# Forgetting attention scores: the product with the keys' rests over 128 partitions in place of 64

## The chip, the cores and the metric
The kernel runs on one core of one Trainium2 chip. The metric is the device time of one execution in microseconds (us), from runs of the whole program; a profile of one further execution shows where the time goes.

## What is computed
The program is a whole small model: a block of forgetting attention ("Fox") with a convolutional feed-forward part, a block of HGRN2 with another, and a second model of retention, stick-breaking attention and a gated feed-forward part. All arithmetic is asked in float32. The change concerns the Fox scores alone:

```python
q = rms_norm(q, q_gain) * hd ** -0.5        # 16 heads of 64, 528 tokens
k = rms_norm(k, k_gain)
s = jnp.einsum('bqhd,bkhd->bhqk', q_blk, k)
s = s + c_blk[..., None] - c[:, :, None, :]
s = jnp.where(q_pos[:, None] >= key_pos[None, :], s, -jnp.inf)
p = jax.nn.softmax(s, axis=-1)
o = jnp.einsum('bhqk,bkhd->bqhd', p, v)
```

## The kernel before
**Splitting.** TensorE takes its operands in a rounded float32 form (fp32r), so a float32 number is kept as a rounded part and a rest, and a dense product is the sum of three: rounded with rounded, rounded with rest, rest with rounded. For the dense layers ScalarE rounds each weight tile (`act_hi`, L404) and VectorE subtracts (`dve_lo`, L408); `pe_group` then issues 48 matmuls for each group of 8 tiles (L445, 128 rows by 128 columns stationary, 264 columns moving; L441 in later stages with 512 columns moving).

**A pair of heads.** The Fox stage runs over 8 pairs of heads. Queries and keys of a pair stand as 128 partitions: head 0 in the lower 64, head 1 in the upper 64. `q_p[:, b, :]` holds for head b its rounded queries on the head's own 64 partitions and their rests on the other 64 (`query_parts`, L1814 to L1821, VectorE). `k_p[:, b, :]` holds the rounded keys of head b on both halves (`key_parts`, L1240, four copies on ScalarE recorded at L1146). So one product over 128 partitions gives (rounded query + query rest) times rounded key. `k_l` holds the rests of the keys (`key_rest`, L1823 to L1827, VectorE), each head's on its own half.

**The scores of a head.** `scores(i, b)` (L753) makes 17 matmuls: for five blocks of query rows (four of 128, one of 16) the product with `k_p` at L766 over 128 partitions, the product with `k_l` at L768 over the 64 partitions of the head, and one at L770 that adds the mask on the diagonal. The last block's keys are split in two runs. The lengths of the moving operand are 128, 256, 384 and 512 for the full blocks, and 128 and 400 for the last. TensorE issues a weight load with every matmul, whether or not the stationary operand is the same as before.

**Order.** TensorE runs a pair as: transposes of the values (L696), dense group 0 of the next pair, `scores(i, 0)`, group 1, `scores(i, 1)`, group 2, `turned(0)` (transposes at L780), group 3, `fox_out(0)` (L684, L688), `turned(1)`, sums for the norms (`fox_sums`, L749), `fox_out(1)`. The last pair has one dense group in all, after both heads' scores. VectorE reads the scores from PSUM, adds the decay and finds each row's minimum (`least`, L1860), ScalarE takes the exponential (L1274), and VectorE normalises (L1872) and empties PSUM (L1877). At a pair's end VectorE scales the next queries and keys (`qk_scaled`, L1811), makes `q_p`, gates the output (`o_t`, L1914 and L1915), then makes `k_s` and `k_l`, and at last the output's rest (`yl`, L1921). ScalarE makes `k_p`, then the rounded output (`yh`), then the transposed values (`v_t`, L1146), then rounds the next weights. `scores(i, 0)` waits for `k_p`, `k_l`, `v_t` and the output of the pair before (semaphores `qk_hi`, `qk_lo`, `vt_ready`, `o_done`). Each engine takes its instructions in the order written.

Of the kernel before, what the change touches and what calls it, by code (L numbers as in the profile page):

```python
# [15 lines left out]
F32 = mybir.dt.float32  # L16
F32R = mybir.dt.float32r
BF16 = mybir.dt.bfloat16
U8 = mybir.dt.uint8
ALU = mybir.AluOpType  # L20
# [3 lines left out]
P = 128  # L24
# [3 lines left out]
L = SEQ + META  # L28
# [8 lines left out]
FOX_H, FOX_D = 16, 64  # L37
# [128 lines left out]
def program(nc, ctx, dram, out):  # L166
# [53 lines left out]
    a = Area(arena, end)  # L220
# [5 lines left out]
    a = Area(arena, end)  # L226
# [12 lines left out]
    a = Area(arena, end)  # L239
# [6 lines left out]
    k_s = a.take("k_s", [P, L])  # L246
# [5 lines left out]

    a = Area(rest, end)
    q_p, k_p = (a.take(n, [P, 2, L], F32R) for n in ("q_p", "k_p"))
    k_l = a.take("k_l", [P, L], F32R)
    ident_f, future_f = (a.take(n, [P, P], F32R) for n in ("ident_f", "future_f"))

    a = Area(rest, end)
# [22 lines left out]
    a = Area(arena, end)  # L281
# [13 lines left out]
    a = Area(after_yr, end)  # L295
    b = Area(norms_at, arena)
# [18 lines left out]
    flat = ps[:, :, :].rearrange("p b n -> p (b n)")  # L315
# [4 lines left out]
    def s(name):  # L320

        if name not in sems:
            sems[name] = ctx.enter_context(nc.semaphore(name))
        return sems[name]
# [376 lines left out]
    def _(pe):  # L701
        pe.wait_ge(s("square_loaded"), 16)
        pe.wait_ge(s("m_loaded"), 32)
        for n in range(2):
            for m in range(KT):
                last = nc.tensor.transpose(ps[:, 3, P * n + META * m:P * n + META * (m + 1)],
                                           m_tok[:, n, P * m:P * (m + 1)], ident[0:META, 0:META])
        last.then_inc(s("x_t"), 1)
        for c in range(NFULL):
            pe.wait_ge(s(f"x_loaded{c}"), 16)  # L710
            for g in range(2):
                b = 2 * c + g
                if b >= 4:
                    pe.wait_ge(s("h_init"), b - 2)
                for m in range(4):
                    last = nc.tensor.transpose(ps[:, 4 + b % 4, P * m:P * (m + 1)],
                                               x_tok[:, c, P * (4 * g + m):P * (4 * g + m + 1)], ident)
# [3 lines left out]
        for l in range(2):  # L721
            last = nc.tensor.transpose(ps[:, 1 + l, 0:4 * FT], crows[0:4 * FT, l, :], ident[0:4 * FT, 0:4 * FT])
# [29 lines left out]

        def scores(i, b):  # L753

            lo, hi = FOX_D * b, FOX_D * (b + 1)
            before = 0
            for turn in TURNS:
                before += len(turn)
                if b:
                    pe.wait_ge(s("t_min"), 10 * i + before)  # L760
                for n in turn:
                    w = TOK[n]
                    at = 1024 + SCORES0[n]
                    runs = ((0, P * n + w),) if n < NFULL else ((0, P), (P, L))
                    for k0, k1 in runs:
                        nc.tensor.matmul(flat[0:w, at + k0:at + k1], q_p[:, b, P * n:P * n + w],  # L766
                                         k_p[:, b, k0:k1], start=True, stop=False)
                        nc.tensor.matmul(flat[0:w, at + k0:at + k1], q_p[lo:hi, b, P * n:P * n + w],  # L768
                                         k_l[lo:hi, k0:k1], start=False, stop=(k1 <= P * n))
                    last = nc.tensor.matmul(flat[0:w, at + P * n:at + P * n + w], ident_f[:, 0:w],  # L770
                                            future_f[:, 0:w], start=False, stop=True)
                last.then_inc(s("s_done"), 1)
# [357 lines left out]
        for m in range(4, KT):  # L1130
            pe.wait_ge(s("ff_ready"), m + 1)
            for c in range(NFULL):
                last = nc.tensor.transpose(ps[:, 4 + c, P * (m - 4):P * (m - 3)], ff[:, m, P * c:P * (c + 1)], ident)
# [557 lines left out]
    def _(dve):  # L1691
        V = nc.vector
# [116 lines left out]
        def qk_scaled(n, j):  # L1809
            dve.wait_ge(s("qn_r"), 2 * n + j + 1)  # L1810
            V.scalar_tensor_tensor((q_s, k_s)[j][:, :], qk_raw[:, j, :], gains[:, ROW_QGAIN + j:ROW_QGAIN + j + 1],  # L1811
                                   post_t[:, j, :], ALU.mult, ALU.mult).then_inc(s("qn_done"), 1)

        def query_parts(n):  # L1814

            dve.wait_ge(s("qn_done"), 2 * n + 3)
            V.tensor_copy(q_p[lo, 0, :], q_s[lo, :])
            V.tensor_copy(q_p[hi, 1, :], q_s[hi, :]).then_inc(s("qk_lo"), 1)
            dve.wait_ge(s("qk_lo"), 2 * n + 1)
            V.tensor_tensor(q_p[hi, 0, :], q_s[lo, :], q_p[lo, 0, :].bitcast(F32), ALU.subtract)  # L1820
            V.tensor_tensor(q_p[lo, 1, :], q_s[hi, :], q_p[hi, 1, :].bitcast(F32), ALU.subtract)  # L1821

        def key_rest(n):  # L1823

            dve.wait_ge(s("qk_hi"), 2 * n + 1)
            V.tensor_tensor(k_l[lo, :], k_s[lo, :], k_p[lo, 0, :].bitcast(F32), ALU.subtract)
            V.tensor_tensor(k_l[hi, :], k_s[hi, :], k_p[hi, 1, :].bitcast(F32), ALU.subtract).then_inc(s("qk_lo"), 1)  # L1827

        V.tensor_copy(ident_f[:, :], ident)
        V.tensor_copy(future_f[:, :], future)  # L1830
# [20 lines left out]
        def pair_(i, ahead_):  # L1851
            def least(b):
                dve.wait_ge(s(f"crep_loaded{b}"), 16 * i + 16)
                for turn in range(3):
                    dve.wait_ge(s("s_done"), 6 * i + 3 * b + turn + 1)
                    carry(dve, "dve_carry")
                    for n in TURNS[turn]:
                        w, k = TOK[n], P * n + TOK[n]
                        at = 1024 + SCORES0[n]
                        V.tensor_tensor_reduce(out=t_rows[0:w, b, ROWS0[n]:ROWS0[n] + k],  # L1860
                                               in0=flat[0:w, at:at + k], in1=crep[0:w, b, 0:k],
                                               scale=1.0, scalar=3e38, op0=ALU.add, op1=ALU.min,
                                               accum_out=rowmin[0:w, 5 * b + n:5 * b + n + 1]).then_inc(s("t_min"), 1)

            def normalise(b):
                dve.wait_ge(s("p_exp"), 10 * i + 5 * b + 5)
                V.reciprocal(rowinv[:, 5 * b:5 * b + 5], rowsum[:, 5 * b:5 * b + 5]).then_inc(s("fox_step"), 1)
                dve.wait_ge(s("fox_step"), 3 * i + b + 1)
                for n in range(NTT):
                    w, k = TOK[n], P * n + TOK[n]  # L1870
                    tr = t_rows[0:w, b, ROWS0[n]:ROWS0[n] + k]
                    last = V.tensor_scalar(tr, tr, rowinv[0:w, 5 * b + n:5 * b + n + 1], None, ALU.mult)  # L1872
                last.then_inc(s("p_norm"), 1)

            def evacuate(b):
                dve.wait_ge(s("pt_mm"), 2 * i + b + 1)
                V.tensor_copy(p_t[:, 512:1024], ps[:, 3, :]).then_inc(s("pt_b"), 1)  # L1877

            def gate():
                dve.wait_ge(s("gate_exp"), i + 1)  # L1880
                V.tensor_scalar(g_s[:, :], g_s[:, :], 1.0, None, ALU.add).then_inc(s("fox_step"), 1)
                dve.wait_ge(s("fox_step"), 3 * i + 3)
                V.reciprocal(g_s[:, :], g_s[:, :]).then_inc(s("gate_ready"), 1)
            if ahead_:
                split_ahead(dve, dve_lo, PH_FOX, i, 0)
                dve.wait_ge(s("qn_done"), 2 * i + 4)
                scaled_out(PH_FOX, i, 0, qk_raw[:, 0, :])
            least(0)
            if ahead_:
                split_ahead(dve, dve_lo, PH_FOX, i, 1)  # L1890
                normalise(0)
                scaled_out(PH_FOX, i, 1, qk_raw[:, 1, :])
                least(1)
                split_ahead(dve, dve_lo, PH_FOX, i, 2)
                normalise(1)
                scaled_out(PH_FOX, i, 2, v_s[:, :])
                evacuate(0)
                split_ahead(dve, dve_lo, PH_FOX, i, 3)
                scaled_out(PH_FOX, i, 3, g_s[:, :])
            else:  # L1900
                least(1)
                split_ahead(dve, dve_lo, PH_FOXG, 0, 0)
                normalise(0)
                scaled_out(PH_FOXG, 0, 0, g_s[:, :])
                normalise(1)
                evacuate(0)
            gate()
            evacuate(1)
            if ahead_:
                qk_scaled(i + 1, 0)  # L1910
                query_parts(i + 1)
            dve.wait_ge(s("o_mm"), 2 * i + 2)
            dve.wait_ge(s("gate_ready"), i + 1)
            V.tensor_tensor(o_t[:, 0:SEQ], ps[:, 5, :], g_s[:, 0:SEQ], ALU.mult)  # L1914
            V.tensor_tensor(o_t[:, SEQ:L], ps[:, 4, 496:512], g_s[:, SEQ:L], ALU.mult).then_inc(s("o_done"), 1)  # L1915
            if ahead_:
                qk_scaled(i + 1, 1)
                key_rest(i + 1)
            dve.wait_ge(s("o_done"), i + 2)
            dve.wait_ge(s("yh_ready"), i + 1)  # L1920
            V.tensor_tensor(row(yl, i), o_t[:, :], row(yh, i).bitcast(F32), ALU.subtract).then_inc(s("y_ready"), 1)  # L1921
# [425 lines left out]
```

## Time and profile before

| | us |
|---|---|
| median of 3 runs | 2983.41 |
| lowest and highest | 2978.47, 2984.93 |
| the profiled execution | 2975.36 |
| its span, first to last instruction | 2973.7 |
| TensorE matmul, busy | 2879.0 |
| TensorE weight load, busy | 2512.3 |
| VectorE, busy | 1493.8 |
| ScalarE, busy | 1122.1 |

The mean granted TensorE clock was 0.982 of full speed. Busy time of TensorE counts modelled ends of overlapping matmuls, so the distance from one matmul's start to the next one's start says more than a duration. PE is TensorE's matmul side, PEld its weight loads, DVE VectorE, ACT ScalarE. "128*128 128x264" is a stationary operand of 128 rows and 128 columns and a moving one of 264 columns. "issue" as the end of an idle time means that the engine waited for nothing that the profile shows.

### The profile page before, as it was taken

To read this page: it belongs to the slowest core of one execution; us is meant where nothing else is said; L and a number is where in the kernel's file an instruction comes from. 1 tells how busy PE (TensorE), PEld (TensorE's weight loads), DVE (VectorE), ACT (ScalarE), POOL (GpSimd) and SP (SyncE) were. 2 spreads that over 40 slices of the span, in tenths; PEclk is the share of its full clock that TensorE was granted. 3 is DMA by queue.
4 is the path that set the end of the run, shared out by engine and by line. 5 is a ranking of instruction groups with operands and counts; after the bars stand their busy time and mean duration, and the time that the engine had idled before them with its cause. 6 is when DMAs were issued, how large, how long until landed. Compare 5 with 4: busy or idle time off the path is not lost.

```text
span 2973.7 us, 46538 instructions
## 1 busy us (share of the span) xinstructions
PE 2879.0 (97%) x17851; PEld 2512.3 (84%) x17851; DVE 1493.8 (50%) x2152; ACT 1122.1 (38%) x1795; POOL 211.2 (7%) x177
## 2 busy tenths in 40 slices
PE   7999999999989999799999999999999999799998
PEld 7888789999989999699987888787788777588886
DVE  6666645554357776555533454353433335544422
ACT  4444434333245554333323233233344444423232
POOL 1000010000112221100001011011000000200000
PEclk9999989999999999899999999999999999899999
DMA  4222113323231111233333322322211112233332
GB/s 126 56 70 54 53 50 92 92 87 90 88 101 50 56 49 45 59 95 92 91 92 101 88 82 72 92 79 60 84 51 49 49 50 79 62 95 96 90 92 74
DMA packets 419559, 225.63 MB, mean 76 GB/s; under 512 B 7589, under 2 KB 416422, under 8 KB 419350
## 3 DMA queue, kind: packets, MB, share of 16 engines
q1 hardware_dynamic: 416438, 211.45, 24.5%
q0 software_dynamic: 2256, 10.32, 1.2%
q10 hardware_dynamic: 784, 2.75, 0.3%
q8 instruction: 55, 0.90, 0.1%
q14 instruction: 26, 0.21, 0.0%
HBM read 222.36 MB, written 2.13 MB: 75 GB/s over the span
## 4 chain that ended last, share of the span: by engine, by line
PE 62%; DVE 4%; issue 2%; ACT 1%; POOL 0%; DVEq 0%; ACTq 0%; POOLq 0%
PE ps L441 34%; PE ps L445 17%; PE ps L1046 2%; PE ps L862 2%; PE ps L1004 1%; PE ps L1067 1%; PE ps L1035 1%; PE ps L971 1%; DVE wl L408 1%; PE ps L907 1%; PE ps L1039 0%; DVE h L526 0%; DVE rl L2187 0%; DVE xl L475 0%; PE ps L896 0%
## 5 line engine op out<-in xcount | busy, mean ns | idle before, releaser
L408 DVE TENSOR_TENSOR wl<-raw,wh 128x1024 fp32r<-128x1024 f32 (+4 forms) x429 | 519.3, 1210 | 401.9 <-ACT wh L404 398.1
L404 ACT ACTIVATE wh<-raw 128x1024 fp32r<-128x1024 f32 (+4 forms) x429 | 428.5, 999 | 727.8 <-PE ps L441 393.4
L445 PE MATMUL ps<-xh,wh 128*128 128x264 f32 x2736 | 573.6, 291 | 14.3 <-DVE xl L475 5.5
L445 PE MATMUL ps<-xl,wh 128*128 128x264 f32 x2736 | 561.7, 287 | 0.0
L445 PE MATMUL ps<-xh,wl 128*128 128x264 f32 x2736 | 561.0, 287 | 0.0
L445 PEld LDWEIGHTS ps<-xh,wh 128*128 128x128 f32 x2736 | 432.4, 191 | 23.8 <-issue 7.3
L445 PEld LDWEIGHTS ps<-xl,wh 128*128 128x128 f32 x2736 | 429.4, 190 | 0.0
L445 PEld LDWEIGHTS ps<-xh,wl 128*128 128x128 f32 x2736 | 428.0, 190 | 0.0
L441 PE MATMUL ps<-xh,wh 128*128 128x512 f32 x976 | 392.0, 402 | 17.9 <-DVE xl L475 14.2
L441 PE MATMUL ps<-xl,wh 128*128 128x512 f32 x976 | 387.8, 397 | 0.0
L441 PE MATMUL ps<-xh,wl 128*128 128x512 f32 x976 | 385.6, 395 | 0.0
L441 PEld LDWEIGHTS ps<-xh,wh 128*128 128x128 f32 x976 | 184.3, 189 | 67.0 <-DVE xl L475 13.4
L441 PEld LDWEIGHTS ps<-xh,wl 128*128 128x128 f32 x976 | 184.7, 189 | 42.0
L441 PEld LDWEIGHTS ps<-xl,wh 128*128 128x128 f32 x976 | 184.4, 189 | 41.5 <-issue 1.7
L441 PE MATMUL ps<-hidh,wh 128*128 128x512 f32 x352 | 138.8, 394 | 0.4 <-DVE wl L408 0.4
L441 PE MATMUL ps<-hidh,wl 128*128 128x512 f32 x352 | 138.9, 395 | 0.0
L441 PE MATMUL ps<-hidl,wh 128*128 128x512 f32 x352 | 138.1, 392 | 0.0
L1730 DVE TENSOR_TENSOR pre<-ps,rstd 128x528 f32<-128x528 f32 (+1 forms) x66 | 46.4, 703 | 171.1 <-PE ps L445 110.4
L1730 DVE TENSOR_TENSOR t<-ps,rstd 128x512 f32<-128x512 f32 (+1 forms) x66 | 46.0, 697 | 145.7 <-PE ps L441 103.9
L486 POOL TENSOR_TENSOR ssq<-ssq,sq 128x528 f32<-128x528 f32 (+1 forms) x56 | 81.9, 1463 | 394.3 <-ACT sq L471 289.7
L1730 DVE TENSOR_TENSOR rt<-ps,rstd 128x512 f32<-128x512 f32 (+1 forms) x53 | 37.0, 697 | 140.2 <-PE ps L441 100.6
L488 POOL COPY ssq<-sq 128x528 f32<-128x528 f32 (+1 forms) x8 | 7.0, 874 | 1402.4 <-ACT sq L471 1143.2
(320 smaller groups left out, 4041.3 us busy)
## 6 DMA issues: line engine op xcount, KB each, us to landing
raw<-in_w_in SPq DMA_DIRECT2D x88, 512.0 KB, 4.0
raw<-in_ffn_w_gate SPq DMA_DIRECT2D x44, 512.0 KB, 3.8
raw<-in_ffn_w_up SPq DMA_DIRECT2D x44, 512.0 KB, 3.8
raw<-in_w_ffn_in SPq DMA_DIRECT2D x44, 512.0 KB, 3.8
raw<-in_fox_w_in SPq DMA_DIRECT2D x33, 512.0 KB, 4.1
raw<-in_hgrn_w_in SPq DMA_DIRECT2D x32, 512.0 KB, 4.0
raw<-in_ffn_w_down SPq DMA_DIRECT2D x32, 448.0 KB, 3.4
raw<-in_ffn_w_down SPq DMA_DIRECT2D x16, 512.0 KB, 3.7
```

The costliest lines, as they stand in the source:

```text
L404: nc.scalar.activation(wh[:, v % 2, 0:nk, :], raw[:, v % RAW_SLOTS, 0:nk, :], ACT.Copy).then_inc(s("w_hi"), 1)
L408: nc.vector.tensor_tensor(wl[:, v % 2, 0:nk, :], raw[:, v % RAW_SLOTS, 0:nk, :], wh[:, v % 2, 0:nk, :].bitcast(F32), ALU.subtract).then_in ...
L441: last = nc.tensor.matmul(ps[:, bank, 0:SEQ], w[:, slot, kk, :], x[:, k0 + k, META:L], start=first, stop=end_)
L445: last = nc.tensor.matmul(ps[:, bank + b, 0:HALF], w[:, slot, kk, :], x[:, k0 + k, b * HALF:(b + 1) * HALF], start=first, stop=end_)
L486: nc.gpsimd.tensor_tensor(ssq[:, t0:L], ssq[:, t0:L], sq[:, m % 2, t0:L], ALU.add).then_inc(s("sq_used"), 1)
L862: last = nc.tensor.matmul(ps[:, 2 + k % 2, P * c:P * (c + 1)], left[:, P * c:P * (c + 1)], right[:, P * c:P * (c + 1)], start=True, stop=True)
L907: last = nc.tensor.matmul(flat[:, at:at + TOK[j]], g_left[:, j * (j - 1) // 2 + c, :], g_f[:, P * j:P * j + TOK[j]], start=True, stop=True)
L971: last = nc.tensor.matmul(flat[0:TOK[j], at:at + SEQ - QFIRST[j]], rt[:, 2 + c, P * j:P * j + TOK[j]], rt[:, c, META + QFIRST[j]:L], start ...
L1004: last = nc.tensor.matmul(ps[:, 4 + e, QFIRST[j]:SEQ], r_vt[0:k, j, P * e:P * (e + 1)], r_s[0:k, QSTRIP[j]:QSTRIP[j] + SEQ - QFIRST[j]], s ...
L1035: nc.tensor.matmul(flat[:, QSTRIP[j]:QSTRIP[j] + SEQ - QFIRST[j]], s_k[lo:hi, P * j:P * j + P], s_q[lo:hi, QFIRST[j]:SEQ], start=(j < 3), ...
L1046: return nc.tensor.matmul(dst, w[:, :], src, start=False, stop=last, skip_group_check=True)
L1730: return V.tensor_tensor(shown(ph, gj, dst), out_of(ph, gj), shown(ph, gj, rstd[:, :]), ALU.mult)\
```

## The change
The product with the keys' rests uses the whole of `q_p[:, b, :]` as stationary operand, the same as the product before it. For that, `k_l` gets a place for each head, with the head's rests on both halves of the partitions; `key_rest` makes it with four subtractions in place of two. The rest times rest product is added to the sum by this. In the pair's end, VectorE scales the keys (`qk_scaled(i + 1, 1)`) before it gates the output, and no longer after. `k_l` grows by 528 columns.

```diff
-    k_l = a.take("k_l", [P, L], F32R)
+    k_l = a.take("k_l", [P, 2, L], F32R)
...
-                        nc.tensor.matmul(flat[0:w, at + k0:at + k1], q_p[lo:hi, b, P * n:P * n + w],
-                                         k_l[lo:hi, k0:k1], start=False, stop=(k1 <= P * n))
+                        nc.tensor.matmul(flat[0:w, at + k0:at + k1], q_p[:, b, P * n:P * n + w],
+                                         k_l[:, b, k0:k1], start=False, stop=(k1 <= P * n))
...
-            V.tensor_tensor(k_l[lo, :], k_s[lo, :], k_p[lo, 0, :].bitcast(F32), ALU.subtract)
-            V.tensor_tensor(k_l[hi, :], k_s[hi, :], k_p[hi, 1, :].bitcast(F32), ALU.subtract).then_inc(s("qk_lo"), 1)
+            for b, own_ in enumerate((lo, hi)):
+                for half in (lo, hi):
+                    last = V.tensor_tensor(k_l[half, b, :], k_s[own_, :], k_p[own_, b, :].bitcast(F32), ALU.subtract)
+            last.then_inc(s("qk_lo"), 1)
...
                 query_parts(i + 1)
+                qk_scaled(i + 1, 1)
             dve.wait_ge(s("o_mm"), 2 * i + 2)
             dve.wait_ge(s("gate_ready"), i + 1)
             V.tensor_tensor(o_t[:, 0:SEQ], ps[:, 5, :], g_s[:, 0:SEQ], ALU.mult)
             V.tensor_tensor(o_t[:, SEQ:L], ps[:, 4, 496:512], g_s[:, SEQ:L], ALU.mult).then_inc(s("o_done"), 1)
             if ahead_:
-                qk_scaled(i + 1, 1)
                 key_rest(i + 1)
```

## Rows read from the trace of the kernel before

**Rows 1.** The page's first part: busy us (share), instructions.

```profile
PE 2879.0 (97%) x17851; PEld 2512.3 (84%) x17851; DVE 1493.8 (50%) x2152; ACT 1122.1 (38%) x1795; POOL 211.2 (7%) x177
```

**Rows 2.** Waits of PE, 50 to 405 us, the longest: total us, times, longest.

```profile
PE ps L766 <- ACT v_t L1146: 7.1, 2, 5.5
```

**Rows 3.** Timeline of PE within one call of scores: start us, us, instruction.

```profile
107.47 0.45 PE L766 MATMUL ps<-k_p,q_p 128*128 128x512 f32 x1
107.84 0.49 PE L768 MATMUL ps<-k_l,q_p 64*128 64x512 f32 x1
108.27 0.33 PE L770 MATMUL ps<-future_f,ident_f 128*128 128x128 f32 x1
108.43 0.39 PE L766 MATMUL ps<-k_p,q_p 128*128 128x384 f32 x1
```

**Rows 4.** Timeline of PEld in the same call.

```profile
107.41 0.19 PEld L766 LDWEIGHTS ps<-k_p,q_p 128*128 128x128 f32 x1
107.84 0.18 PEld L768 LDWEIGHTS ps<-k_l,q_p 64*128 64x128 f32 x1 [0.25 <-issue]
108.26 0.19 PEld L770 LDWEIGHTS ps<-future_f,ident_f 128*128 128x128 f32 x1 [0.24 <-issue]
```

**Rows 5.** Timelines elsewhere: wide dense matmuls, transposes, loads of 16 rows after 128.

```profile
2700.21 0.39 PE L441 MATMUL ps<-xl,wh 128*128 128x512 f32 x1
2700.44 0.39 PE L441 MATMUL ps<-xh,wl 128*128 128x512 f32 x1
...
99.61 0.77 PE L696 MATMUL ps<-square,v_s 128*128 128x128 f32 x5
100.13 0.49 PE L445 MATMUL ps<-xh,wh 128*128 128x264 f32 x2
...
127.31 0.33 PEld L780 LDWEIGHTS ps<-square,t_rows 16*128 16x128 f32 x5 [0.17 <-issue]
```

**Rows 6.** Stretches of PE: window, us, busy (x), clock, DMA, GB/s; sums of 14, 4.

```profile
106.08:110.17 4.09, 4.09 (x19) 1.00 0.11 27
149.69:154.12 4.43, 4.43 (x19) 0.90 0.19 37
sum 58.30, PE 58.30; mean PE 4.16
...
110.19:116.15 5.96, 5.96 (x51) 1.00 0.24 72
sum 28.01, PE 28.01; mean PE 7.00
...
371.76:385.34 13.58, 13.58 (x34) 0.50 0.00 1
385.34:392.81 7.47, 7.47 (x50) 0.77 0.24 71
```

**Rows 7.** Timeline, end of a pair and start of the next.

```profile
141.49 0.64 ACT L503 ACTIVATE post_t<-post_t 128x528 f32<-128x528 f32 x1
...
143.33 0.70 DVE L1821 TENSOR_TENSOR q_p<-q_s,q_p 64x528 fp32r<-64x528 f32 x1
...
144.74 0.76 DVE L1811 SCALAR_TENSOR_TENSOR k_s<-qk_raw,gains,post_t 128x528 f32<-128x528 f32 x1
145.53 2.63 ACT L1146 ACTIVATE k_p<-k_s 64x528 fp32r<-64x528 f32 x4 [3.39 <-DVE k_s L1811]
...
148.73 0.73 ACT L1146 ACTIVATE v_t<-ps 128x512 f32<-128x512 f32 x2
...
149.69 0.30 PE L766 MATMUL ps<-k_p,q_p 128*128 128x128 f32 x1
...
150.44 1.23 DVE L408 TENSOR_TENSOR wl<-raw,wh 128x1024 fp32r<-128x1024 f32 x1 [0.67 <-ACT wh L404]
```

**Rows 8.** Timeline, the first pair up to its scores.

```profile
58.93 0.70 DVE L1826 TENSOR_TENSOR k_l<-k_s,k_p 64x528 fp32r<-64x528 f32 x1 [1.37 <-ACT k_p L1146]
...
61.09 0.30 PE L766 MATMUL ps<-k_p,q_p 128*128 128x128 f32 x1 [1.60 <-ACT v_t L1146]
```

More of the change, by code:

```diff
@@ L753, in scores @@
         def scores(i, b):
-            lo, hi = FOX_D * b, FOX_D * (b + 1)
             before = 0
```

## The prediction, made before the changed kernel was built
> **What bounds the kernel now.** I read the page's first part before anything else: TensorE is busy 2879.0 of 2973.7 us, VectorE half of that and ScalarE 1122.1 [rows 1]. Then the waits of TensorE in the Fox stage, since the change lives there alone: in 355 us the costliest wait is 7.1 us in two pieces for the transposed values `v_t`, one of them 5.5 us, and nothing recurs in every pair [rows 2]. So in the Fox stage TensorE's own stream of instructions is the clock, with two exceptions: the starts of the first and of the last pair. The third view is the timeline of one call of `scores`, read by distances between starts. A product over 512 columns with the rounded keys starts at 107.47, the one with the rests at 107.84, the mask at 108.27: 0.37 and 0.43 us. The mask's own 128 columns take 0.16 until 108.43 [rows 3]. Dense matmuls of 512 columns, accumulating into one bank, follow each other in 0.23 us [rows 5]. So each wide product in the scores costs 0.14 to 0.20 us more than its width asks.
>
> The weight loads say why. The load for L766 at 107.41 is taken while the mask product is still under way, but the load of the 64-row operand comes with its matmul at 107.84 after 0.25 us of "issue", and the 128-row load behind it at 108.26 after 0.24 us [rows 4]. At both changes of height the load isn't taken ahead. The loads of 16 rows behind transposes of 128 rows show the same idle time, 0.17 us, in code of another kind [rows 5]. A call has 6 products over 64 rows, so 6 changes down and 6 up, and lasts 4.09 us at full clock [rows 6].
>
> The Trainium skill has a sentence for this ("TensorEngine Tiling (Array Packing)", Key Properties): changing the tiling mode, unlike changing tiles within it, drains TensorE. The rows agree with it: 0.24 and 0.25 us of idle load side at the two changes.
>
> **The change, part by part.**
>
> *Product over 128 rows.* All 17 matmuls of a call then have full height. I price each by a distance between full-height neighbours: 0.23 us for 512 columns, and 0.10 for 128 (five transposes in 0.52 us) [rows 5]; 48 matmuls of 264 columns in 5.96 us give 0.124 [rows 6]. Between 264 and 512 that is 0.43 ns a column, so 0.12 for 256, 0.18 for 384 and 0.18 for 400. For 128 I take 0.11. First block: three of 0.11, 0.33. Second: two of 0.12 and a mask, 0.35. Third full width: 0.46 + 0.11 = 0.57. The one of 384: 0.36 + 0.11 = 0.47. Last block: 0.22 + 0.36 + 0.04 = 0.62. Sum 2.34 us. The upper bound adds the mask's present 0.16 [rows 3] four times in place of 0.11, 0.2 us; if loads of the last block stay awkward, 2.6 in all. The lower bound is the pure streaming rate, 4144 columns at 0.45 ns (0.23 us for 512), 1.9; with the narrow ones bounded by their loads, 2.0.
>
> *Fourteen calls.* The calls of the first seven pairs take 58.30 us together [rows 6]; four of them contain a fall of the clock to half, such as 4.43 us at mean clock 0.90. After: 14 x 2.34 = 32.8. Gain 25.5.
>
> *Clock.* In four places the granted clock is at its lower level (1.2 GHz) after a call of scores had filled the time before it, and the dense group that follows takes 7.00 us in the mean, 28.01 for the four, against 5.96 for one at full clock [rows 6]. What TensorE did before each fall was these broken-up matmuls; with them closed up I expect no fall. Gain 28.01 - 4 x 5.96 = 4.2. Lower bound zero.
>
> *Last pair.* Both its calls run at clock 0.50 after the 5.5 us wait and take 13.58 us, and the group behind them 7.47 at 0.77 [rows 2, 6]. The wait stays at about 5 us, so I expect the low clock at first. A low-clock call cost 6.79 against 4.09, a ratio of 1.66, so an unbroken one would cost 3.9; two at low clock 7.8, two at full clock 4.7. I take the clock to come back on the way, 6.6, and the group at 5.96. Gain 7.0 + 1.5 = 8.5. Bounds: 5.8 (7.8 and no help to the group) and 10.4.
>
> *VectorE's two more subtractions, and the earlier scaling.* One subtraction takes 0.70 us [rows 8], so `key_rest` grows from 1.4 to 2.8. In a pair's end: the second query rest ends at 144.03. `k_s` (0.76) then comes ahead of the output's gating, which costs no wait, as its input was ready at 141.49 + 0.64 = 142.13. It ends at 144.8 rather than 145.5, and ScalarE's whole chain (`k_p`, `yh`, `v_t`) moves 0.7 forward, `v_t` from 149.46 to 148.8. The gating ends at about 145.6, long before ScalarE comes to `yh` at 147.5. `key_rest` may begin after two of four copies of `k_p` (1.3 us, so at 146.15) and ends at 148.97. The scores start at 149.69, when the dense group is through [rows 7]. So 0.7 us is left, where 0.23 was left before (for `v_t`), and the two subtractions are hidden behind the dense group of 5.96 us. Behind `key_rest` on VectorE stands `yl`, which ends near 149.7, as ScalarE's `yh` no longer keeps it waiting, and then the weights' rest for group 1. That ended at 151.67 [rows 7]; the rounding before it is 0.7 earlier, so now about 151.0. TensorE will ask for it at 149.69 + 2.34 = 152.0. This is what is late next, with 1 us to spare. Without the earlier scaling 0.36 us would be left. `least`, the exponentials and the later splits follow the calls of scores and have the next dense group of 5.96 us for cover. No DMA and no queue of SP or POOL is moved past.
>
> *First pair.* Its order is unchanged, and the scores started at 61.09, after `v_t`. `key_rest` starts at 58.93 and now ends at 58.93 + 2.8 = 61.75, so the scores start near 61.8 [rows 8]. Loss 0.7. *Last pair's start:* there the scores start as `v_t` lands (shape as in rows 7); now `k_l` is last, 0.5 earlier than `v_t` was. Gain 0.5.
>
> Sum: 25.5 + 4.2 + 8.5 - 0.7 + 0.5 = 38.0 us. The profiled execution took 2975.36, so 2937.4; the median of the runs shown is 8.05 higher, 2983.41, which gives 2945.4.
>
> **The rivals.**
>
> *Only part of the stall goes* (chance 0.08). The product with the rests adds onto the sum that the product before has just written; the load might wait for that and not for the height. Then 0.14 us stays at 6 places of 16 calls, 13 us: 2959. Against it: the wide dense matmuls accumulate in one bank at 0.23 us [rows 5].
>
> *Nothing goes* (0.05). The stationary operand is the same, and if the load had to wait for its rows of the array to be free, full height would never overlap. A page of the Trainium skill ("TensorE: Matmul & The Clock Gate", What overlaps and what doesn't) says that loads overlap running matmuls only when the row group differs; by it alone full height would gain nothing, 2983. The trace is against it as it stands: full-height loads do run under full-height matmuls in the load at 107.41 [rows 4] and at 0.124 us for 264 columns [rows 6]. The time of this rival is 2983.4 + 0.7 - 0.5 = 2983.6.
>
> *VectorE's chain becomes the bound, slower* (0.02). The scaled keys now stand ahead of the gating. If the keys' norm came later than 144.03, `o_t`, `yh` and `v_t` would slip with it, and the next scores wait for them. It decides from 1.9 us of delay of `post_t` on (142.13 against 144.03), or from 0.7 us more of `key_rest`. The price, with the stalls left: 0.76 less the present 0.23 of slack, 0.5 us in seven pairs, and 0.7 at the first, and two more falls of the clock at 1.0 us each (7.00 less 5.96): some 6 us, 2990. The slack speaks against it, and so does that norm and queue both keep their distance to TensorE.
>
> **How the numbers follow.** The forecast has 0.85, and 2945 is its time. The range's upper end: 2.6 us for 2.34 in 14 calls (3.6), the clock's 4.2 not returned, the last pair at its bound (2.7), the highest run 1.5 above the median: 2957.4; the partial rival lies at 2959, so 2960. The lower end: 2.0 us a call (4.8), the last pair 1.9 better, and the lowest run 4.9 under the median: 2933.8, so 2933. A measurement of this kernel tells 0.2% (6 us) from no change. Faster by over that: 0.85 + 0.08 = 0.93. Within it: 0.05. Slower: 0.02.
>
> **What would show it.** In the profile after: L768 with 128 rows; the weight load behind it no longer "issue" idle; a call of scores near 2.3 us; dense groups after scores all near 5.96; two calls of the last pair below 8 us; `k_l` in four pieces of 0.70, with no wait of L766 for VectorE save in the first and last pair. It is wrong if a call stays above 3 us, if L766 waits for `k_l` in every pair, or if L445 begins to wait for `wl`. Falls of the clock at other places would cost about 1 us each.

## The result, and the profile after
The changed kernel takes 2934.07 us (median of 4 runs, 2933.94 to 2936.32), the kernel before 2980.94 us in the runs beside it (4 runs, 2977.71 to 2984.93). The ratio is 0.9851, 95% interval 0.9837 to 0.9865: 47 us, or 1.5%, less. On two other chips, where both kernels ran again beside each other, it was 42 us: 2976.80 to 2934.86 and 2975.64 to 2933.95 (ratios 0.9852 and 0.9858). The profiled execution took 2934.11 us against 2975.36, 41.3 us less. The forecast was 2945, with a range of 2933 to 2960: right in sign and cause; the time came out 11 us below the forecast, 1 us above the lower end of the range.

The first part of the page after (busy us, share, instructions) answers to [rows 1]. TensorE has as many instructions as before and is 39 us less busy; VectorE has 16 more, the two subtractions of eight pairs.

```profile
PE 2839.7 (97%) x17851; PEld 2501.2 (85%) x17851; DVE 1501.4 (51%) x2168; ACT 1120.2 (38%) x1795; POOL 210.7 (7%) x177
```

The matmul timeline within one call of scores after (start us, us, instruction), which answers to [rows 3]. L766, L768 and L770 are now L765, L767 and L769.

```profile
144.53 0.28 PE L767 MATMUL ps<-k_l,q_p 128*128 128x256 f32 x1
144.65 0.22 PE L769 MATMUL ps<-future_f,ident_f 128*128 128x128 f32 x1
144.71 0.45 PE L765 MATMUL ps<-k_p,q_p 128*128 128x512 f32 x1
144.99 0.40 PE L767 MATMUL ps<-k_l,q_p 128*128 128x512 f32 x1
145.23 0.22 PE L769 MATMUL ps<-future_f,ident_f 128*128 128x128 f32 x1
145.28 0.39 PE L765 MATMUL ps<-k_p,q_p 128*128 128x384 f32 x1
```

And its weight loads, to be set beside [rows 4].

```profile
144.76 0.19 PEld L767 LDWEIGHTS ps<-k_l,q_p 128*128 128x128 f32 x1
145.00 0.19 PEld L769 LDWEIGHTS ps<-future_f,ident_f 128*128 128x128 f32 x1
145.23 0.19 PEld L765 LDWEIGHTS ps<-k_p,q_p 128*128 128x128 f32 x1
```

From the 512-column product with the rounded keys to the next block's first product there were 0.96 us (107.47 to 108.43) and now there are 0.57 (144.71 to 145.28). The load at 144.76 starts 0.23 us ahead of its matmul at 144.99, and the one at 145.00 0.23 us ahead of 145.23. The loads at 107.84 and 108.26 had started together with theirs. No "issue" stands before these loads any more.

The stretches after (window, us, PE busy, clock, DMA share, GB/s): an ordinary call, the sum of the fourteen calls of the first seven pairs, then a dense group, the two calls of the last pair, and the group behind them. They answer to [rows 6].

```profile
104.28:106.45 2.17, 2.17 (x19) 1.00 0.00 0
...
sum 31.72, PE 31.72; mean PE 2.27
...
106.46:112.40 5.94, 5.94 (x51) 1.00 0.32 88
342.52:349.30 6.78, 6.77 (x35) 0.67 0.01 2
349.30:355.23 5.93, 5.93 (x51) 1.00 0.30 89
```

The waits of TensorE from 50 to 405 us (total, times, longest), which answer to [rows 2]: still two, and they now end with `k_l` on VectorE and not with `v_t`.

```profile
PE ps L765 <- DVE k_l L1827: 7.6, 2, 5.2
PE ps L749 <- DVE v_s L1729: 1.8, 1, 1.8
```

The end of a pair after, against [rows 7]: `k_s` ahead of the gating (`o_t`), four subtractions in one row, and the scores 0.66 us behind their end (140.56 + 2.85 = 143.41).

```profile
138.43 0.77 DVE L1810 SCALAR_TENSOR_TENSOR k_s<-qk_raw,gains,post_t 128x528 f32<-128x528 f32 x1
139.11 0.68 DVE L1916 TENSOR_TENSOR o_t<-ps,g_s 128x512 f32<-128x512 f32 x1
...
140.56 2.85 DVE L1827 TENSOR_TENSOR k_l<-k_s,k_p 64x528 fp32r<-64x528 f32 x4 [0.69 <-ACT k_p L1145]
...
142.42 0.73 ACT L1145 ACTIVATE v_t<-ps 128x512 f32<-128x512 f32 x2
...
144.07 0.22 PE L765 MATMUL ps<-k_p,q_p 128*128 128x128 f32 x1
```

Where the 41.3 us of the two profiled executions went: from the first dense matmul to the end of the Fox stage 387.24 us became 349.96, 37.3 less. What follows took 2568.85 and takes 2565.14, 3.7 less with the same instructions. The last 0.3 lie in the start. The two stretches, first before, then after:

```profile
17.61:404.85 387.24, 372.83 (x2493) 0.95 0.22 58
404.85:2973.70 2568.85, 2497.71 (x15310) 0.99 0.26 77
```

```profile
17.30:367.26 349.96, 334.88 (x2493) 0.97 0.24 64
367.26:2932.40 2565.14, 2496.78 (x15310) 0.99 0.26 77
```

### The profile page after: what moved, and what is told of

It reads as the page before. It is cut to its first block, busy times and chain, and to the rows that moved or that the text cites. A ratio compares the mean times of both kernels' runs of the same rounds, so it can differ in the third digit from the quotient of the medians.

```text
span 2932.4 us, 46554 instructions
## 1 busy us (share of the span) xinstructions
PE 2839.7 (97%) x17851; PEld 2501.2 (85%) x17851; DVE 1501.4 (51%) x2168; ACT 1120.2 (38%) x1795; POOL 210.7 (7%) x177
## 4 chain that ended last, share of the span: by engine, by line
PE 63%; DVE 5%; issue 2%; ACT 1%; POOL 0%; DVEq 0%; ACTq 0%; POOLq 0%
PE ps L441 34%; PE ps L445 17%; PE ps L1045 2%; PE ps L861 2%; PE ps L1003 1%; PE ps L1066 1%; PE ps L1034 1%; PE ps L970 1%; DVE wl L408 1%; PE ps L906 1%; PE ps L1038 0%; DVE h L526 0%; DVE rl L2188 0%; DVE xl L475 0%; PE ps L895 0%
## 5 line engine op out<-in xcount | busy, mean ns | idle before, releaser
L408 DVE TENSOR_TENSOR wl<-raw,wh 128x1024 fp32r<-128x1024 f32 (+4 forms) x429 | 518.5, 1209 | 400.5 <-ACT wh L404 397.0
L445 PE MATMUL ps<-xh,wh 128*128 128x264 f32 x2736 | 569.7, 289 | 13.4 <-DVE xl L475 6.0
L445 PE MATMUL ps<-xl,wh 128*128 128x264 f32 x2736 | 557.9, 285 | 0.0
L445 PE MATMUL ps<-xh,wl 128*128 128x264 f32 x2736 | 557.5, 285 | 0.0
L445 PEld LDWEIGHTS ps<-xh,wh 128*128 128x128 f32 x2736 | 428.4, 189 | 24.1 <-issue 6.1
L445 PEld LDWEIGHTS ps<-xl,wh 128*128 128x128 f32 x2736 | 425.6, 189 | 0.0
L445 PEld LDWEIGHTS ps<-xh,wl 128*128 128x128 f32 x2736 | 424.4, 189 | 0.0
```

The lines of the kernel that those rows point to most:

```text
L408: nc.vector.tensor_tensor(wl[:, v % 2, 0:nk, :], raw[:, v % RAW_SLOTS, 0:nk, :], wh[:, v % 2, 0:nk, :].bitcast(F32), ALU.subtract).then_in ...
L445: last = nc.tensor.matmul(ps[:, bank + b, 0:HALF], w[:, slot, kk, :], x[:, k0 + k, b * HALF:(b + 1) * HALF], start=first, stop=end_)
```

## The experiments
Theory: each change between stationary operands of different height keeps TensorE from loading the next operand ahead, and the change removed twelve of these in each of sixteen calls. The rivals: the 64-row products are slow as such; the load is cheap now because the operand is in the array already; the earlier scaling of the keys, or the new place of `k_l`, brought part of the gain. Four kernels ran on one chip, where the kernel before took 2976.80 us.

### The 64-row product alone put back

```diff
-                        nc.tensor.matmul(flat[0:w, at + k0:at + k1], q_p[:, b, P * n:P * n + w],
-                                         k_l[:, b, k0:k1], ...)
+                        nc.tensor.matmul(flat[0:w, at + k0:at + k1], q_p[64 * b:64 * b + 64, b, P * n:P * n + w],
+                                         k_l[64 * b:64 * b + 64, b, k0:k1], ...)
```

> The changed kernel with the product with the keys' rests back on the head's own 64 rows; four subtractions, both places of k_l and the earlier scaling stay. Theory (the gain is the change of height alone): the calls of scores are 4.0 to 4.1 us again, some falls of the clock come back, and the time is within 2 us of the kernel before, near 2980. Rival (the earlier scaling, or the second place of k_l, brought part of the gain): below 2970.

Measured: 2977.70 us, ratio to the kernel before 0.9999 (0.9990 to 1.0009). Its stretches show the old call, and with it the low clock in five of the fourteen calls, of which one is shown:

```profile
110.65:114.69 4.04, 4.04 (x19) 1.00 0.25 65
154.20:158.49 4.29, 4.29 (x19) 0.91 0.33 82
```

So the gain comes with the height of one product: with that alone taken back, the median is the kernel before's within 3 us. Beside the long calls, the 16 more subtractions and the earlier scaling come to nothing that the median shows. What the earlier scaling is worth once the calls are short is another question, taken up below.

### All three products on 64 rows

```diff
-    ... q_p[:, b, P * n:P * n + w], k_p[:, b, k0:k1] ...
-    ... q_p[:, b, P * n:P * n + w], k_l[:, b, k0:k1] ...
-    ... ident_f[:, 0:w], future_f[:, 0:w] ...
+    ... q_p[64 * b:64 * b + 64, b, P * n:P * n + w], k_p[64 * b:64 * b + 64, b, k0:k1] ...
+    ... q_p[64 * b:64 * b + 64, b, P * n:P * n + w], k_l[64 * b:64 * b + 64, b, k0:k1] ...
+    ... ident_f[64 * b:64 * b + 64, 0:w], future_f[64 * b:64 * b + 64, 0:w] ...
```

> All three products of the scores on the head's own 64 rows: the product of the queries' rests with the rounded keys and half of the mask are left out, the number and widths of the matmuls stay. Theory (a change of height is what stalls, not 64 rows as such): a call has one change at its start and one at its end in place of twelve within, and takes 2.2 to 2.6 us; the time is 2935 to 2941. Rival (a 64-row load is never taken ahead, whatever stands before it): each load waits, a call takes 4 us or more, the time is 2975 or more.

Measured: 2942.29 us, ratio 0.9877 (0.9859 to 0.9894). A call, the dense group behind it and the next call in its stretches, and then the loads and matmuls of one block:

```profile
104.16:106.49 2.33, 2.33 (x18) 1.00 0.00 0
106.49:112.61 6.12, 6.12 (x50) 1.00 0.30 86
112.61:114.96 2.35, 2.35 (x19) 1.00 0.76 208
```

```profile
104.90 0.44 PE L765 MATMUL ps<-k_p,q_p 64*128 64x512 f32 x1
104.95 0.19 PEld L767 LDWEIGHTS ps<-k_l,q_p 64*128 64x128 f32 x1
105.18 0.39 PE L767 MATMUL ps<-k_l,q_p 64*128 64x512 f32 x1
105.19 0.18 PEld L769 LDWEIGHTS ps<-future_f,ident_f 64*128 64x128 f32 x1
```

A 64-row load behind a 64-row matmul is taken 0.23 us ahead (104.95 for 105.18) like a full one: 64 rows are not slow. What is left over the changed kernel sits at the ends of a call, 2.34 for 2.17 and 6.12 for 5.94, 0.35 us for one change down and one up where a call meets a dense group. Fourteen times that is 4.9 us. In the last pair the two calls stand side by side; they and the group behind them take 15.68 us against 12.78, the calls at mean clock 0.50 against 0.63. The Fox stage of the profile is 357.43 us against 350.51 for the changed kernel run again, 6.9 more, and the medians on this chip stand 7.4 apart (2942.29 and 2934.86). The calls are within the 2.2 to 2.6 us expected, the time is 1.3 us above its range.

### Half as many changes of height

The next two, and the first run of the head-by-head version below, were on another chip, with the kernel before at 2975.25 us. The changed kernel itself did not run on that chip.

```diff
+                        order = {0: "FMR", 1: "RFM", 2: "RFM", 3: "FMR", 4: "FR" if k0 == 0 else "RFM"}[n]
+                        for x in order:
+                            last = nc.tensor.matmul(*parts[x], start=x == order[0], stop=x == order[-1])
```

F is the product with the rounded keys on 128 rows, R the one with the rests on 64, M the mask. The blocks run in the order 0, 1, 3, 2, 4, so that R ends one block and opens the next.

> The product with the rests on 64 rows as before the change, but the order of the products alternates from block to block (rounded, mask, rest; then rest, rounded, mask), so that two products over 64 rows stand side by side: 3 changes of height down and 3 up in a call instead of 6 and 6; the matmuls, their shapes and what they add are those of the kernel before. Theory (each change of height stalls by itself): a call takes half way between 2.17 and 4.05 us, 3.1, and the time is some 15 us above the changed kernel, 2950 to 2957 with whatever falls of the clock remain. Rival (each 64-row product costs by itself): a call stays at 4.05 and the time at 2977.

Measured: 2953.94 us, ratio 0.9930 (0.9913 to 0.9946). Two of its calls in its stretches:

```profile
103.54:106.60 3.06, 3.06 (x19) 1.00 0.08 16
112.54:115.59 3.05, 3.05 (x19) 1.00 0.75 211
```

And two of its weight loads: a pair of 64-row products is loaded, and then the 128-row product behind it. In the whole call there are three such places down and three up.

```profile
104.95 0.29 PEld L772 LDWEIGHTS ps<-k_l,q_p 64*128 64x128 f32 x2 [0.19 <-issue]
105.55 0.19 PEld L772 LDWEIGHTS ps<-k_p,q_p 128*128 128x128 f32 x1 [0.31 <-issue]
```

With 12, 6 and 0 changes a call takes 4.04, 3.06 and 2.17 us: 0.98 for the first six that go, 0.89 for the last six, so 0.15 to 0.16 us for one change. The same matmuls with the same shapes in another order give half of the gain in a call. That is the strongest of the tests: against the kernel with the 64-row product alone put back only the order differs, and with it which product opens the sum in PSUM.

### Another stationary operand of full height

```diff
-                        nc.tensor.matmul(flat[0:w, at + k0:at + k1], q_p[:, b, P * n:P * n + w],
+                        nc.tensor.matmul(flat[0:w, at + k0:at + k1], q_p[:, 1 - b, P * n:P * n + w],
```

> The changed kernel with the other head's queries as stationary operand of the product with the keys' rests, over 128 rows: the rest's share of the scores comes out as another one, all shapes stay. Theory (height alone): calls of 2.17 us, time 2934, within 3 us. Rival (the load is cheap because the same operand is in the array already): the load before each product with the rests costs its full time again, a call takes 2.8 us or more, the time is 2943 or more.

Measured: 2939.63 us (2931.95 to 2940.89), ratio 0.9872 (0.9852 to 0.9892). A call and a group in its stretches:

```profile
103.09:105.28 2.19, 2.19 (x20) 1.00 0.00 0
105.28:111.22 5.94, 5.94 (x51) 1.00 0.32 88
```

A call takes 2.19 us where the changed kernel has 2.17: that the operand is the same is worth 0.02 us a call, if anything. The median missed the bound (2931 to 2937) by 2.6 us, and the call doesn't explain that. In the profiled execution (2940.00 us) the Fox stage takes 350.73 us, close to the changed kernel's 348.87 to 350.51, and what follows, the same instructions, takes 2570.21 against 2565.14 to 2567.59, with the clock low for some 80 us in place of 66 to 77. Its one run at 2931.95 and the three near 2940 are the spread taken up under "What stays open".

### The earlier scaling of the keys taken back

```diff
                 query_parts(i + 1)
-                qk_scaled(i + 1, 1)
...
             if ahead_:
+                qk_scaled(i + 1, 1)
                 key_rest(i + 1)
```

> The changed kernel with the scaling of the keys put back behind the gating of the output. Theory (TensorE's stream is the clock, the vector chain has slack): k_l then ends near 149.7 in the frame of the old trace, just as the dense group before the scores ends, so six of the seven pair starts keep their time or lose up to 0.1 us; the last pair's start, where nothing covers the chain, loses 0.7 us. In all 1 to 2 us slower than the changed kernel, near 2935.5. Rival (the four subtractions set the start of the scores, and the move hides them): each of seven pairs waits 0.5 us or more for k_l, and the time is 2939 or more.

> The changed kernel once more, to stand beside the variant without the move on the same chip. Both theories: 2934, within 3 us.

Measured: 2940.78 us (2939.25 to 2942.55) beside 2934.86 (2932.55 to 2939.89) for the changed kernel: 5.9 us, not 1 to 2. The time is one that the rival gave (2939 or more), the waits are not. In its trace the dense group ahead of a pair's scores, and the call itself, are longer, since `k_l` lands as the group ends and the load isn't taken ahead:

```profile
135.41:141.53 6.12, 6.12 (x51) 1.00 0.00 0
141.53:143.79 2.26, 2.26 (x18) 1.00 0.00 0
```

Against 5.96 and 2.18 (138.11 to 144.07 and 144.07 to 146.25) that is 0.24 us, 1.4 in six pairs; with the last pair's 0.7 it makes 2.1. So the waits lie at the places that were forecast and are far from the rival's 0.5 in each pair, but each costs 0.24 us where at most 0.1 was expected, and more than half of the measured difference is outside them. I ran it again beside its base on a third chip (the kernel before at 2975.64 us there).

> The variant without the earlier scaling again, beside its base on one chip. It was 5.9 us slower than the base before, where 1 to 2 was expected; its Fox stage was 3 us longer in the profile. Theory (0.24 us at six pair starts, 0.7 at the last, and the rest falls of the clock): the Fox stage is 2 to 4 us longer, the median 2 to 6 us above the base. Rival (the move has a cost of its own in every pair that the profile shows elsewhere): the stage is 5 us longer or more.

> The changed kernel, as the base of the two beside it on this chip: 2932 to 2937.

Measured: 2937.53 us (2935.30 to 2939.12) beside 2933.95 (2932.79 to 2937.21), 3.6 us. The windows of the Fox stage and of all that follows, first of this variant, then of its base:

```profile
18.08:367.86 349.78, 334.17 (x2492) 0.98 0.24 64
367.86:2937.40 2569.54, 2498.59 (x15310) 0.99 0.26 77
```

```profile
17.51:366.38 348.87, 334.39 (x2493) 0.98 0.24 64
366.38:2932.50 2566.12, 2498.07 (x15310) 0.99 0.26 77
```

The stage itself is 0.9 us longer in this pair of profiles and 2.7 in the first (353.24 against 350.51), one below and one within the 2 to 4 expected; the rival's 5 is excluded. The two profiled executions are 4.9 us apart (2939.12 and 2934.22): 0.9 in the stage, 0.6 ahead of it, and 3.4 behind it, in instructions that are the same in both. The difference of the medians, 3.6, is within the 2 to 6 expected, but falls of the clock do not account for it in these profiles: behind the stage the clock is low for some 70 us in both. Of the 3.4 us, 2.5 are in two rows of TensorE's waits there, 11.6 against 10.4 us for the weights' rests (`wl`, L408) and 4.2 against 2.9 us of "issue" before L445. Why they grew isn't shown.

### Head by head, a version meant to be faster
ScalarE copies the values before the keys' parts; both engines make head 0's parts first, and the scores of head 0 wait for these alone.

```diff
-            pe.wait_ge(s("qk_hi"), 2 * i + 2)
-            pe.wait_ge(s("qk_lo"), 2 * i + 2)
+            pe.wait_ge(s("qk_hi"), 4 * i + 2)
+            pe.wait_ge(s("qk_lo"), 2 * i + 1)
             scores(i, 0)
...
+            pe.wait_ge(s("qk_hi"), 4 * i + 4)
+            pe.wait_ge(s("qk_lo"), 2 * i + 2)
             scores(i, 1)
...
                 qk_rsqrt(i + 1)
+                values(i + 1)
                 key_parts(i + 1)
...
                 qk_scaled(i + 1, 0)
-                query_parts(i + 1)
+                query_parts(i + 1, 0)
                 qk_scaled(i + 1, 1)
...
-                key_rest(i + 1)
+                key_rest(i + 1, 0)
+                query_parts(i + 1, 1)
+                key_rest(i + 1, 1)
```

> The changed kernel with the work of a pair's end put head by head: ScalarE copies the transposed values before the keys' rounded parts, both copies of head 0's keys come first, VectorE makes head 0's query rest, then (after the gating) head 0's key rests, then head 1's; scores of head 0 wait for head 0's parts alone. Theory (TensorE waits for this chain only at the first and the last pair, 2.4 and 5.2 us): the first wait goes nearly, the last falls to about 2.5 us, and with a shorter wait the low clock behind it is shorter; 5 to 9 us less than the changed kernel, 2926 to 2930. Rival (the waits are set by something else, or shorter waits only move): within 2 us of 2934.5.

> The head-by-head order again, beside its base on one chip. In its first profile TensorE reached the end of the Fox stage 7.3 us earlier than in the changed kernel, but the median time was only some 1 us lower. Theory (the stage gain is real, and falls of the clock in later stages, which land elsewhere when the stages start earlier, add or take some us in each run): the Fox stage is again about 7 us shorter, and the median 3 to 7 us lower than the base, with single runs closer. Rival (later stages take the gain back by a wait of their own): the stage is shorter and the median within 1.5 us of the base, with a new wait in a later stage.

Measured: 2933.86 us (2929.99 to 2935.24), ratio 0.9861 (0.9845 to 0.9878), and on the third chip 2934.61 (2926.76 to 2935.35), ratio 0.9852 (0.9836 to 0.9869), beside 2933.95 of its base. Its waits in the second profile, and its stretches:

```profile
PE ps L765 <- DVE k_l L1831: 2.9, 1, 2.9
```

```profile
18.20:361.96 343.76, 333.34 (x2492) 0.98 0.24 65
361.96:2927.60 2565.64, 2497.13 (x15310) 0.99 0.26 77
```

The two waits of 7.6 us became one of 2.9, and the Fox stage is 5.1 us shorter than its base's 348.87, as meant. The profiled executions are at 2929.99 and 2929.24 us. Of the nine executions in all, three are below 2930 and six between 2933.7 and 2935.4, where the base lies. The gain forecast for the median did not come, neither 5 to 9 us nor, in the second run, 3 to 7: both medians are where the rivals had put them (within 2 and within 1.5 us of the base). But the second rival's cause, a new wait in a later stage, isn't in the profile. The version beats the kernel before; that it beats the changed one isn't shown.

## Why the prediction was right
**What bounds the stage.** Right. TensorE's stream set the time: its matmuls are 38.0 us less busy in the stage (372.83 to 334.88), and the stage is 37.3 us shorter.

**The stall and its cause.** Right, and shown by the tests: the height of the one product taken back takes the gain with it, 64 rows alone don't cost, order alone moves it, another full-height operand keeps the gain. The rival "nothing goes" fell with the trace after, where full-height loads run 0.23 us ahead of full-height matmuls. The sentence of the Trainium skill ("TensorE: Matmul & The Clock Gate", What overlaps and what doesn't) that loads overlap only when the row group differs would have had it so; here the measurement decides against it. "Only part of the stall goes" fell with the load at 144.76, taken ahead although its matmul adds onto the sum that is being written. The Trainium skill's sentence on the drain at a change of tiling mode ("TensorEngine Tiling (Array Packing)", Key Properties) agrees with the loss at each change of height, 12, 6 and 0 in a call. It gives no price, and a change in the number of columns alone, from 128 to 16, shows no such loss (0.06 us from the mask at 145.68 to the next product at 145.74).

**Fourteen calls.** 25.5 us foretold, 58.30 - 31.72 = 26.6 measured. A call was priced at 2.34 us and takes 2.17. The blocks from the call at 144.07, priced and measured: 0.33 and 0.28, 0.35 and 0.36, 0.57 and 0.57, 0.47 and 0.46, 0.62 and 0.51. So the term that was off is the last block, and a little the first. I gave each of its two 128-column products 0.11, the price with a stationary operand of 128 columns; with one of 16 columns they take 0.06:

```profile
145.74 0.22 PE L765 MATMUL ps<-k_p,q_p 128*16 128x128 f32 x1
145.80 0.22 PE L767 MATMUL ps<-k_l,q_p 128*16 128x128 f32 x1
145.86 0.34 PE L765 MATMUL ps<-k_p,q_p 128*16 128x400 f32 x1
```

In the wide blocks the price of the mask, 0.11, held only as part of a sum: the mask's start is 0.05 ahead of the next product's (145.23 to 145.28), and the 512-column product behind a mask takes 0.28 in place of 0.23 (144.71 to 144.99). Thirteen calls gained 2.2 us over the forecast by the lower price; the first gave 1.1 back, as it ran at mean clock 0.62 and took 3.47.

**Clock.** 4.2 us foretold, 3.9 measured: the four groups of 28.01 us became 6.29 and three of 5.94. Between 68 and 340 us the clock isn't lowered once. With the old product put back it was lowered in five of the fourteen calls, with half of the changes (calls of 3.06 us) in none. From the second pair to the seventh it fell only in the two kernels with twelve changes in a call. At the first and the last pair, behind TensorE's waits, it fell with short calls too: the first call of the changed kernel ran at mean clock 0.62, which the sum did not have.

**Last pair.** 8.5 foretold, 13.58 + 7.47 - 6.78 - 5.93 = 8.3 measured, at mean clock 0.67 in the calls. An unbroken call at the low clock was put at 3.9 us; the two on 64 rows, all at clock 0.50, take 7.70. The start gained 0.3 of the 0.5.

**VectorE.** The slack of `k_l` was put at 0.7 us and is 0.66; no L765 waits for it but at the first and the last pair. The first pair's dense group with its wait grew from 7.70 to 8.54 us, 0.8 for the 0.7 foretold. The rival of a vector chain that decides did not come, and the variant without the earlier scaling shows how near it was: with one operation of 0.76 us later it costs 0.24 us at each of six pair starts. The prediction had 0.36 us of slack left without the earlier scaling, and that was wrong: 0.7 less 0.76 is nothing, and in the trace of that variant `k_l` ends at 141.38, when a group of 5.96 us begun at 135.41 is through.

**What the sum lacked.** It gave 38.0 us from one profiled execution to the other, and the Fox stage, for which it was made, is 37.3 shorter. Its terms as measured come to 38.3; the part of the stage ahead of the dense group before the first scores, where nothing changed, took 1.2 longer in the trace after (17.30 to 54.29 against 17.61 to 53.39), which has a fall of the clock at 28 to 34 us that the one before hasn't. From one execution to the other 41.3 were measured. 3.7 lie behind the Fox stage, where nothing changed. Three profiles of the changed kernel itself take 2565.14, 2566.12 and 2567.59 us there, and those of the variants (span less the end of the stage) up to 2570.2, with the stretches of low clock in other places. I had counted such differences into the range only as spread of the runs. The rest of the distance from 2945 is the base: I added 38 to a median of three runs, 2983.41, which with the later runs is 2980.94 and in the three later comparisons 2975.25 to 2976.80. Had I gone by the profile alone, 2937.4, the miss would be 3.3 us. So of the 11 us between forecast and median, 8 are the base that I chose, and that the median still lay in the range is owed in part to the range's width.

**What stays open.** Why a program whose Fox stage is 5 us shorter has most of its executions where the base's are, and why the variant with the other operand has three of four at 2940. The mean granted clock of each execution is on record, and within a kernel the longer executions mostly have the lower one. Of the nine head-by-head executions the three below 2930 us have 0.986 or 0.987, the six others 0.983 to 0.985. With the other operand the three near 2940 have 0.982 or 0.983, the one at 2931.95 has 0.986. The changed kernel's three longest, 2939.89, 2937.21 and 2937.15, have 0.983, its four shortest 0.986. In the profiles the low clock of the later stages lies at other places and for other lengths from run to run. So most of the spread goes with the clock. Why an execution gets the lower mean is not shown, nor whether stages which begin at another time meet it differently: the profile took one execution of each, and in both cases of the head-by-head order one of the three shortest.

## What to carry to other kernels
Look at TensorE by distances between starts, and at the weight loads for "issue" idle behind a matmul of another height: there the next operand isn't loaded ahead, whatever its width. The sign is a load that starts together with its own matmul; "issue" alone is not, as the loads of L684, all of 128 rows, have it 71 times in the trace after. A product over half of the rows among full ones is then dearer than a full one with useful or harmless rows in the other half; where it can't be filled, put the short ones side by side, which here halved the loss for nothing. And before adding work to the engine that feeds the next stage, work out the slack in the frame of the trace: here one operation of 0.76 us moved forward left 0.66 us of slack behind 1.4 us of added work, and without the move there was none.

## What the runs showed of the hardware beyond what was expected
One change of height, 128 rows to 64 or back, costs 0.15 to 0.16 us between matmuls of 16 to 512 columns in a call (4.04, 3.06, 2.17 us at 12, 6 and 0 changes), and 0.35 us for the two where a call on 64 rows lies between dense groups. A 128-column product on a stationary operand of 128 columns costs 0.11 us among its like (144.13 to 144.24), on one of 16 columns 0.06. Behind a 512-column product it starts only 0.05 ahead of the next one, but that next wide product then takes 0.05 longer, 0.28 for 0.23.
